# Queries and keys of the last recurrent stage: three reduced-precision passes over upper and lower parts in place of the native float32 product

## What is computed

```python
xc = conv_b + xpad[:, 0:T] * conv_w[0]
for j in range(1, CONV_K_3):
    xc = xc + xpad[:, j:j + T] * conv_w[j]
xc = jax.nn.silu(xc)
xch = xc.reshape(B, T, M_HEADS, M_HD)
q = jnp.einsum('bthd,hde->bhte', xch, wq)
k = jnp.einsum('bthd,hde->bhte', xch, wk)
...
h = mlstm_chunkwise(q, k, v, im.transpose(0, 2, 1), (fm + f_bias).transpose(0, 2, 1))
```

## Time and profile before

| what | us |
| --- | --- |
| median of three runs | 2837.55 (2837.01 to 2837.66) |
| the profiled execution, whole | 2835.23 |
| its span, first to last instruction | 2833.4 |
| TensorE busy | 2805.0 (99% of the span) |
| VectorE busy | 1400.3 (49%) |
| ScalarE busy | 1065.1 (38%) |
| DMA, mean rate | 124 GB/s |
| the sixty-four records of the native product (L2440), busy | 28.1 |

### The profile page before, as it was taken

The page is one execution under the profiler, slowest core; times in us unless marked ns, Lnnn a source line. Parts: engine busy times, 40 slices in busy tenths (PEclk is TensorE's granted clock), DMA queues, the critical chain, the costliest instruction groups (busy, mean ns, idle before and its releaser), DMA issues.

```text
span 2833.4 us, 38304 instructions
## 1 busy us (share of the span) xinstructions
PE 2805.0 (99%) x15496; PEld 2331.3 (82%) x15496; DVE 1400.3 (49%) x2501; ACT 1065.1 (38%) x1810; POOL 348.3 (12%) x596
## 2 busy tenths in 40 slices
PE   8999999999999999999999999999999999999998
PEld 7888777888889888888888889887778777778888
DVE  6686644436337444555554236335544553445534
ACT  5332233554226333322222236434444543233322
POOL 6457143100001000000000001000000000000011
PEclk9999999999999999999999999999999999999999
DMA  7566354324325545466654325432222223222423
GB/s 203 146 184 132 104 129 120 105 78 151 118 97 183 155 152 153 148 186 186 186 178 156 135 97 134 122 97 68 71 68 72 73 62 96 82 75 82 149 97 119
DMA packets 448161, 350.49 MB, mean 124 GB/s; under 512 B 73373, under 2 KB 403965, under 8 KB 443761
## 3 DMA queue, kind: packets, MB, share of 16 engines
q1 hardware_dynamic: 412818, 241.93, 29.7%
q0 software_dynamic: 35168, 106.10, 12.6%
HBM read 322.88 MB, written 22.81 MB: 122 GB/s over the span
## 4 chain that ended last, share of the span: by engine, by line
PE 96%; DVE 2%; DMA 1%; ACT 1%; issue 0%; POOL 0%; SPq 0%; ACTq 0%; DVEq 0%
PE bank L3583 58%; PE bank L3623 16%; PE bank L3593 4%; PE bank L3646 2%; PE bank L3541 2%; PE bank L2368 1%; PE bank L2419 1%; PE bank L2395 1%; PE bank L2440 1%; PE bank L652 1%; PE bank L2488 1%; PE bank L722 1%; DMA ring<-in_w_in 1%; PE bank L686 0%; PE bank L648 0%; PE bank L2414 0%
## 5 line engine op out<-in xcount | busy, mean ns | idle before, releaser
L3736 DVE TENSOR_TENSOR ring_parts<-ring,ring_hi 128x1024 fp32r<-128x1024 f32 x416 | 506.1, 1228 | 699.1 <-ACT ring_hi L3695 694.1
L3695 ACT ACTIVATE ring_hi<-ring 128x1024 fp32r<-128x1024 f32 (+1 forms) x420 | 437.4, 1050 | 577.1 <-DMA ring<-in_w_in 295.8
L3583 PE MATMUL bank<-A_parts,ring_hi 128*128 128x512 f32 x1552 | 620.6, 400 | 0.2 <-DVE ring_parts L3736 0.2
L3583 PE MATMUL bank<-A_parts,ring_parts 128*128 128x512 f32 x1552 | 606.1, 391 | 0.0
L3583 PE MATMUL bank<-X_parts,ring_hi 128*128 128x512 f32 x1360 | 530.1, 390 | 0.0
L3583 PE MATMUL bank<-B_parts,ring_hi 128*128 128x512 f32 x1224 | 479.2, 391 | 0.0
L3583 PEld LDWEIGHTS bank<-A_parts,ring_hi 128*128 128x128 f32 x1552 | 291.8, 188 | 66.0 <-issue 8.4
L3583 PEld LDWEIGHTS bank<-A_parts,ring_parts 128*128 128x128 f32 x1552 | 291.4, 188 | 62.4
L3583 PEld LDWEIGHTS bank<-X_parts,ring_hi 128*128 128x128 f32 x1360 | 255.7, 188 | 51.2 <-issue 0.5
L3583 PE MATMUL bank<-B_parts,ring_parts 128*128 128x512 f32 x752 | 292.9, 390 | 0.0
L3583 PEld LDWEIGHTS bank<-B_parts,ring_hi 128*128 128x128 f32 x1224 | 230.2, 188 | 52.3 <-issue 5.9
(11 more groups left out here) (571 smaller groups left out, 3879.1 us busy)
## 6 DMA issues: line engine op xcount, KB each, us to landing
ring<-in_w_in SPq DMA_DIRECT2D x288, 512.0 KB, 3.7
ring<-in_w_out SPq DMA_DIRECT2D x96, 512.0 KB, 3.5
work<-in_w_ada POOLq DMA_DIRECT2D x96, 512.0 KB, 4.9
ring<-in_w_in SPq DMA_DIRECT2D x48, 256.0 KB, 3.7
ring<-in_w_mem_kv SPq DMA_DIRECT2D x16, 512.0 KB, 4.1
x_keep<-X POOLq DMA_DIRECT2D x8, 1024.0 KB, 5.0
X<-x_keep POOLq DMA_DIRECT2D x8, 1024.0 KB, 9.9
X<-in_x SPq DMA_DIRECT2D x4, 1024.0 KB, 10.7
```

What stands on the lines that cost most here:

```text
L3583: mm = nc.tensor.matmul(K.ps(st)[0:w + (t["beside"] or 0), 0:t["n"]], lhsT=wp[:, j, :], rhs=columns(ap, kk), start=first, stop=end)
L3695: nc.scalar.activation(slot_view[key](ring_hi), slot_view[key](ring), ACT.Copy).then_inc(s_hi, 1)
L3736: nc.vector.tensor_tensor(lo, slot_view[key](ring), slot_view[key](ring_hi), ALU.subtract).then_inc(s_lo, 1)
```

## The change

`ml_qk` is computed from parts like the tiles. Its slot becomes a split slot. A new stage `xc_parts` for each head writes the upper part of the two convolved tiles with ACT (`xc_hi`) and the lower part with DVE (`xc_lo`). `xc_hi` lies in the memory of `hbuf`, and `xc_lo` in that of `E` and `Pm`; both are free between `ml_t` of a head and `ml_s` of the next, so ACT waits for the transposes of the head before. TensorE then does 24 matmuls in `float32r` for a head in place of 8 native ones. The diff, cut to its core (the table of stages and the declarations of the semaphores are left out):

```diff
     mq, mk = s("mq", 2, SEQ), s("mk", 2, SEQ)
+    xc_lo = K.work_parts[:, s.at[0]:s.at[0] + 2 * SEQ].rearrange("p (k t) -> p k t", t=SEQ)
     E, Pm = s("E", SEQ), s("Pm", SEQ)
...
+    xc_hi = K.work_parts[:, s.at[0]:s.at[0] + 2 * SEQ].rearrange("p (k t) -> p k t", t=SEQ)
     hbuf = s("hbuf", TT, M_HD)
...
-    script += [MZ[3], qk[0], MZ[4], sc[0], MZ[5], num[0], MZ[6], tr[0]]
-    script += [M[2][0], qk[1], M[2][1], sc[1], M[2][2], num[1], M[2][3], M[2][4], tr[1]]
-    script += M[2][5:7] + [("mix_parts", 3, 4), M[2][7], qk[2], M[3][0], sc[2], M[3][1], num[2], M[3][2], tr[2]]
+    xparts = [("xc_parts", h) for h in range(M_H)]
+    script += [xparts[0], MZ[3], qk[0], MZ[4], sc[0], MZ[5], num[0], MZ[6], tr[0], xparts[1]]
+    script += [M[2][0], qk[1], M[2][1], sc[1], M[2][2], num[1], M[2][3], M[2][4], tr[1], xparts[2]]
+    script += M[2][5:7] + [("mix_parts", 3, 4), M[2][7], qk[2], M[3][0], sc[2], M[3][1], num[2], M[3][2], tr[2], xparts[3]]
...
     def pe_ml_qk(pe, st):
         h = st[1]
-        pe.wait_ge(s_xc, 2 * h + 2)
-        pe.wait_ge(*K.slot_loaded(st))
+        pe.wait_ge(s_xc_lo, h + 1)
+        pe.wait_ge(*K.slot_split(st))
         if h == 0:
             pe.wait_ge(s_nsa, len(pairs) // TT)
-        w = K.slot_ap(st).rearrange("p (m k e) -> p m k e", m=2, k=2)
+        hi, lo = (w.rearrange("p (m k e) -> p m k e", m=2, k=2) for w in K.slot_parts(st))
         for m, key in ((0, "q"), (1, "k")):
             for e in range(2):
                 bk.take(pe, st, (key, e))
                 for d in range(2):
-                    mm = nc.tensor.matmul(ps(st, (key, e)), lhsT=w[:, m, d, e * P:(e + 1) * P], rhs=xc[:, 2 * (h % 2) + d, :],
-                                          start=(d == 0), stop=(d == 1))
+                    for n, (w, x_) in enumerate(((hi, xc_hi), (hi, xc_lo), (lo, xc_hi))):
+                        mm = nc.tensor.matmul(ps(st, (key, e)), lhsT=w[:, m, d, e * P:(e + 1) * P], rhs=x_[:, d, :],
+                                              start=(d == 0 and n == 0), stop=(d == 1 and n == 2))
                 mm.then_inc(bk.full_sem(st, (key, e)), 1)
...
+    def act_xc_parts(act, L, st):
+        h = st[1]
+        act.wait_ge(s_xc, 2 * h + 2)
+        if h == 0:
+            act.wait_ge(s_nsa, len(pairs) // TT)
+        else:
+            act.wait_ge(*bk.filled(("ml_t", h - 1), 1))
+        nc.scalar.activation(xc_hi, xc[:, 2 * (h % 2):2 * (h % 2) + 2, :], ACT.Copy).then_inc(s_xc_hi, 1)
...
+    K.split_slots.append("ml_qk")
...
+    def vec_xc_parts(vec, L, st):
+        h = st[1]
+        vec.wait_ge(s_xc_hi, h + 1)
+        nc.vector.tensor_tensor(xc_lo, xc[:, 2 * (h % 2):2 * (h % 2) + 2, :], xc_hi, ALU.subtract).then_inc(s_xc_lo, 1)
...
         def is_split(st, sub):
             if st[0] != "tile":
-                return st[0] in ("wo", "wor")
+                return st[0] in K.split_slots
...
+        K.slot_split = lambda st, sub=0: (s_lo, split_no[st, sub] + 1)
+        K.slot_parts = lambda st, sub=0: (slot_view[st, sub](ring_hi), slot_view[st, sub](ring_lo))
```

More of the change, by code:

```diff
@@ L2170, in block3 @@
     s_xc = K.sem("xc_ready")
+    s_xc_hi, s_xc_lo = K.sem("conv_upper_ready"), K.sem("conv_lower_ready")
     s_E = K.sem("decay_logits_ready")
@@ L3044, in block3 @@
     K.stage("act", final3=act_final, tile3=act_tile, turn=act_turn, mg_rows=act_mg_rows, mg_exp=act_mg_exp, cmp_end=act_cmp_end, cmp2=act_cmp2, nsa_s=act_nsa_s, nsa_t=act_nsa_t, nsa_cs=act_nsa_cs, nsa_ct=act_nsa_ct,
-            ml_qk=act_ml_qk, ml_s=act_ml_s, ml_n=act_ml_n, wo_gate=act_wo_gate)
-    K.stage("vec", tile3=vec_tile, mg_rows=vec_mg_rows, mg_scan=vec_mg_scan, mg_nat=vec_mg_nat, cmp_end=vec_cmp_end, nsa_s=vec_nsa_s, nsa_t=vec_nsa_t,
+            xc_parts=act_xc_parts, ml_qk=act_ml_qk, ml_s=act_ml_s, ml_n=act_ml_n, wo_gate=act_wo_gate)
+    def vec_xc_parts(vec, L, st):
+        h = st[1]
+        vec.wait_ge(s_xc_hi, h + 1)
+        nc.vector.tensor_tensor(xc_lo, xc[:, 2 * (h % 2):2 * (h % 2) + 2, :], xc_hi, ALU.subtract).then_inc(s_xc_lo, 1)
+    K.stage("vec", xc_parts=vec_xc_parts, tile3=vec_tile, mg_rows=vec_mg_rows, mg_scan=vec_mg_scan, mg_nat=vec_mg_nat, cmp_end=vec_cmp_end, nsa_s=vec_nsa_s, nsa_t=vec_nsa_t,
             nsa_w=vec_nsa_w, nsa_cs=vec_nsa_cs, nsa_cw=vec_nsa_cw, nsa_o=vec_nsa_o, ml_s=vec_ml_s, ml_n=vec_ml_n, ml_t=vec_ml_t,
@@ L3067, in __init__ @@
         self.y_base, self.y_count = {}, 0
+        self.split_slots = ["wo", "wor"]
         self.slot_src, self.slot_count, self.slot_used = {}, {"wo": 8}, {}
```

## The result

Over twenty executions each, the median went from 2837.02 us (2834.87 to 2839.78) to 2833.56 us (2831.29 to 2835.04): 3.46 us, a ratio of 0.9987 with a 95% interval of 0.9982 to 0.9993. That is faster, by less than the 0.2% that the prediction took as its line. The forecast was 2833.3 us and a saving of 4.2 us; it started from 2837.55 us, the median of three executions.

A forecast was written before the change was run, and what follows sets the result against it. TensorE, busy 99% of the span, was taken as the bound. Gains of 1.42 + 0 + 1.40 + 1.40 = 4.22 us over heads 0 to 3 took the median from 2837.55 to 2833.3 us, range 2831.2 to 2836.2.

The forecast's parts named there:

- the 0.2% that the prediction took as its line: Whole kernel: about 0.2% (5.7 us) can be told from no change; forecast counted as within it, same 0.84, faster 0.12.
- What bounds the kernel: Whole kernel: TensorE, busy 99% of the span; a change pays only by what it takes from TensorE's stream.
- The gain at a head: ml_qk: 24 passes at 0.2273 us replace the native product, gaining 1.42 us at head 0, 1.40 each at heads 2, 3.
- a pass that isn't 0.227 us: ml_qk: a sign that would prove the prediction wrong; it took 0.2273 us a pass from 96 matmuls of two tiles.
- upper bound, 0.23: ml_qk: longest time allowed for a pass, 0.23 us, from the step of loads just behind the native product.
- The lost gain of head 1: Behind ml_qk of head 1: M[2][1] waits for its weight split after M[2][0]'s Silu, so gain 0, wait about 1.6 us.
- The slack at the other heads: Next tile's first lower weight part ends before TensorE asks: slack 2.3, 1.2 and 1.2 us at heads 0, 2, 3.
- The added work: Copies and subtractions, 8.4 us on ScalarE and 9.8 us on VectorE in all, none on TensorE's path if each fits.
- the bound with the slowest landing: Head 1: weights landing after 4.4 us at worst put the end of xc_lo at 2453.5, slack 4.0 us before ml_qk.
- The whole gain: Rival: head 1 gains too, 5.6 us saved in all, 2831.9 us; chance 0.09.
- Weight loads outside the passes: Rival: ml_qk steps of 0.42 us, 3.1 us slower per head, 2850 us; chance 0.04 together with copies on the path.
- a quarter of 6.87 saved: ml_qk: alternative estimate by the skill's four passes for true FP32, three for four, 1.7 us a head instead of 1.4.

The follow-up runs named there:

- e3: The changed kernel with all its added copies, subtractions and waits, but TensorE multiplies natively in float32 as before: 2836.49 us against 2836.24 before, ratio 1.0000.
- e5: The kernel before (native product) with the two weight splits of M[2][1] placed ahead of M[2][0]: 2836.24 us against 2836.97 before, ratio 0.9997.
- e1: The changed kernel with the two weight splits of M[2][1] placed ahead of M[2][0]: 2831.47 us against 2836.24 before, ratio 0.9982.
- e4: The changed kernel with M[2][1]'s weight splits ahead of M[2][0] and the xc parts moved to columns 3520 and 6176: 2830.79 us against 2836.24 before, ratio 0.9982.

## Why the prediction was right

**What bounds the kernel.** That TensorE's stream sets the time was right: e3 added 18 us of work on other engines (9.2 us on VectorE, 8.7 us on ScalarE) and cost nothing, and the gain of the change is TensorE's own to 0.1 us.

**The gain at a head.** The mechanism held, the size was off, and one of the prediction's own signs of being wrong, a pass that isn't 0.227 us, came true. The step that was mis-sized is the price of a new pass: the prediction took 0.2273 us from two tiles in a row, because form, type and size were the same. It was 5.67 / 24 = 0.236 us. The operand's start address wasn't the same: the tiles' operands start at multiples of 512 columns or at a place rounded to 32, the new buffers at 3513 and 6169. The prediction's own upper bound, 0.23, was too low as well. By its own count head 0 went from 7.33 to 6.13 us, where 5.91 was forecast, and heads 2 and 3 from 7.53 to 6.35 us, where 6.13 was forecast. On three heads this made 3.6 us of the 4.22 forecast.

**How near the median came.** That 2833.3 us missed the measured 2833.56 by only 0.3 us is in part luck. The saving was put 0.76 us too high (4.22 against 3.46), and the start of the sum, a median of three executions, lay 0.53 us above that of twenty. The two errors cancel for the most part. The saving by itself lies well inside the stated 1.6 to 5.2 us.

**The lost gain of head 1.** This held to 0.1 us. The prediction read it from a wait of 0.24 us and a tile of 11.16 in place of 10.89 us, and from the order of the splits; e5 and e1 put 0.28 us and 1.42 us on it. The expected wait of about 1.6 us counts from the end of a product of 5.45 us; with 5.67 about 1.4 is left. The trace has 1.15 us of idle time, mainly because it counts from the end of the last pass, 0.40 us behind its start, and not from where the next one would start, 0.236 us behind it. From the first pass of `ml_qk` to the second matmul of `M[2][1]` it is 2464.66 - 2457.37 = 7.29 us, where the prediction had 7.34.

**The slack at the other heads.** It held: no other tile waited, neither in the changed kernel nor with passes of 0.229 us in e4. At head 2 of the changed kernel the first lower part ends at 2533.67 + 1.23 = 2534.90 us, 1.5 us ahead of the tile; 1.2 us had been computed for shorter passes, and in e4 it is 1.4 us. The timelines of VectorE and of TensorE:

```profile
2533.67 2.36 DVE L3759 TENSOR_TENSOR ring_parts<-ring,ring_hi 128x1024 fp32r<-128x1024 f32 x2 [0.21 <-ACT ring_hi L3718]
...
2536.43 0.40 PE L3606 MATMUL bank<-A_parts,ring_hi 128*128 128x512 f32 x1
```

**The added work.** It lay where the prediction put it. For head 1 the lower part of `xc` was done at 2450.84 + 1.23 = 2452.07 us and `ml_qk` began at 2457.37: 5.3 us of slack, where the bound with the slowest landing gave 4.0. The timeline of VectorE in the changed kernel:

```profile
2444.89 1.23 DVE L3759 TENSOR_TENSOR ring_parts<-ring,ring_hi 128x1024 fp32r<-128x1024 f32 x1 [1.95 <-ACT ring_hi L3718]
...
2450.84 1.23 DVE L3064 TENSOR_TENSOR work_parts<-X,work_parts 128x1024 fp32r<-128x1024 f32 x1
2457.57 0.75 DVE L2722 TENSOR_SCALAR X<-bank,par 128x512 f32<-128x512 f32 x1 [5.50 <-PE bank L3606]
```

The first row is the lower part of head 1's weights, the second that of `xc`, and the third the convolution that must not be held up; 5.50 us lie free between them.

**The rivals.** The whole gain did not arrive with the change; with both edits of e4 it did. Weight loads outside the passes fall: the loads of `ml_qk` are 0.19 us each, and a load and a pass one behind the other would need 0.42 us; the passes are 0.236 us apart. By the rule of the Trainium skill ("TensorE: Matmul & The Clock Gate", The mechanism) that loads overlap with running matmuls only when the row group differs, the change would have lost time; the trace disagrees for this form. The same section also names a load into a background buffer as a case of overlap, and no run shows which case this is. The other rule that was weighed ("FP8 and Floating Point Precision", TensorE Precision Notes, of the Trainium skill: four passes for true FP32) fits the 6.87 us, though the trace has only sixteen records a head, not thirty-two passes. The sum by it, a quarter of 6.87 saved, was too high by 0.5 us a head; it counts passes and knows nothing of their pitch.

## What to carry to other kernels

Here a product in three reduced-precision passes took a sixth to a fifth less time than the native float32 product (5.67 or 5.50 against 6.87 us). It pays if the parts can be made where ScalarE and VectorE are idle. Before counting such a gain, look at what the next stage on TensorE waits for: where a chain through other engines ends at the same moment, the gain only becomes a wait, and moving work of an in-order engine ahead of a blocked instruction can get it back. Start a `float32r` buffer that TensorE streams from at a multiple of 32 elements; it costs up to 31 columns of memory and gave 0.17 us in 5.67.

## What the runs showed of the hardware

- A `float32r` pass of 512 columns took 0.236 us with its moving operand at an odd column, 0.232 at multiples of 16, 0.229 at multiples of 32. The float32 products of the scores (2.80 and 1.79 us) showed no such effect when their moving operand went from column 1465 to 1472.
- Weight loads of 0.19 us for 128x128 lay under other passes, and not between them: load and pass together came every 0.229 to 0.236 us.
- After 6.8 us without a matmul TensorE resumed at a granted clock of 0.50 (1.2 GHz) and had it back within 6 us, which cost 2.68 us on top of the wait. After 1.15 us without one the clock stayed at 1.00.
